# A two-block transformer kernel: projections spread evenly over the stick-breaking stream, gate rows made by transfers, and the second half's squares moved into the stream

## The chip, the cores and the metric

The kernel runs on one core of one Trainium2 chip. The metric is device time in microseconds, lower is better. TensorE (PE) multiplies, VectorE (DVE) and ScalarE (ACT) do the element-wise work, GpSimd (POOL) splits some weights, and SyncE (SP) issues most transfers.

## What is computed

Two transformer blocks are run one after the other on 1024 rows of width 1024. The first one has pooling, sliding-window attention, a feed-forward part and a gate. The second one is the one that matters here, and within it the stick-breaking attention and the mixing:

```python
def stick_breaking_attention(q, k, v):
    ...
        logits = jnp.einsum("bqhd,bkhd->bhqk", q[:, q_start:k_end],
                            k[:, :k_end]).astype(jnp.float32) * scale
        strict = (q_start + jnp.arange(SB_BLOCK))[:, None] > jnp.arange(k_end)[None, :]
        log_beta = jax.nn.log_sigmoid(logits)
        log_keep = jnp.where(strict, jax.nn.log_sigmoid(-logits), 0.0)
        log_tail = lax.cumsum(log_keep, axis=3, reverse=True) - log_keep
        weights = jnp.where(strict, jnp.exp(log_beta + log_tail), 0.0).astype(v.dtype)
        outs.append(jnp.einsum("bhqk,bkhd->bqhd", weights, v[:, :k_end]))

def hybrid_layer(x, c_act, w_ada, b_ada, w_in, rel_bias, g_a, g_b, w_out, ...):
    mod = c_act @ w_ada + b_ada
    shift_mix, scale_mix, gate_mix, shift_ffn, scale_ffn, gate_ffn = jnp.split(mod, N_MOD, axis=-1)
    h = modulate(rms_norm(x), shift_mix, scale_mix)
    proj = h @ w_in
    ...
    mixed = jnp.concatenate([rms_norm(oa) * g_a, rms_norm(ob) * g_b], axis=-1) @ w_out
    x = x + gate_mix[:, None, :] * mixed
    h = modulate(rms_norm(x), shift_ffn, scale_ffn)
    ...
    x = x + gate_ffn[:, None, :] * ((jax.nn.silu(gate) * val) @ w_down)
```

`oa` is a banded attention of 8 heads, `ob` the stick-breaking attention of 8 heads. `gate_mix` and `gate_ffn` are one number per output column, so the kernel needs them as rows that stand in all 128 partitions.

## The kernel before

Every engine has its own program, written out by hand; the order of work is the order of the code, and semaphores join the engines. A float32 product is made of three passes over operands that were split into a high and a low part (`passes`, lines 792 to 794): high by high, high by low, low by high. ScalarE or GpSimd makes the high part, VectorE subtracts to make the low part.

**The banded attention** (`outputs2`, `turn2`, `scores2`) runs 64 steps. Beside it `jobs2` computes the projections of the next pair of heads, by the table `PLAN_A`.

**The stick-breaking attention** runs NS = 96 steps, NB = 24 for each of four pairs of heads (pair 0 is steps 0 to 23, pair 3 steps 72 to 95). A step is one block of 128 queries by 128 to 512 keys for one head. In step s TensorE turns the weights of step s-2 (`turn3`, line 1355), multiplies those of step s-4 with the values (`outputs3`, lines 1371 and 1373), then does the filler work of the step, and in odd steps computes the logits of the next two (`scores3`, line 1340). ScalarE takes two sigmoids (`signs`) and copies the turned weights (`turned_hi`, wt_hi). VectorE runs a scan and a product for step s-1 (`tails`, lines 2436 and 2440) and subtracts for step s-3 (`turned_lo3`, line 2445, wt_lo). So one thing waits on another in a ring: logits, sigmoids, scan, transpose, copy, subtraction, output.

**The filler in steps 0 to 71** is the projection of the next pair (`jobs2` with `PLAN_B`): 48 products for a pair, each three matmuls over 512 columns, and two transposes (kind T) that turn the columns of V. `PLAN_B = job_plan(JOBS2, 0, 21, NB)` puts the 48 products into the first 21 of 24 steps, in the order V, Q, K, and T into steps 22 and 23. `job_hi` (ACT) and `job_lo` (DVE) copy each finished half out.

**The filler in steps 72 to 96** (`beside3`) is the first half of the mixing. In step 72 `spread_gate` multiplies `diag` (16 diagonal blocks that VectorE makes in step 71, line 2490) by ones, which leaves `gate_mix` as a row in all partitions; ScalarE copies it to `mix_gate`. In steps 73 to 76 TensorE turns eight blocks of `oa` (`turn_mixed`, line 1389), in steps 77 to 92 it multiplies (`first_half_row`, 16 pieces of 12 matmuls), and VectorE scales and adds (`first_half_sum`, lines 2478 and 2481). The mixing's weights are split by `mix_weight_hi` and `mix_weight_lo` (line 2469) in steps 70 to 73 and 93 to 96, four each, and four more blocks are turned in steps 93 to 96.

**After step 99** the second half of the mixing follows: `second_row(0)` and `(1)`, four blocks turned, a second `spread_gate` for `gate_ffn`, `second_row(2)` to `(7)`, while ScalarE squares the rows of `ob` (`ob_square`, line 1914), takes a root (line 1920) and VectorE a reciprocal (`rsq_b`). `second_sum(r)` (line 2538) needs `rsq_b` and frees the PSUM buffer that `second_row(r+2)` fills.

## Time and profile before

| what | value |
|---|---|
| median of 3 runs | 2686.29 us (2685.44 to 2689.0) |
| the profiled execution, its own time | 2674.91 us |
| its span in the trace | 2673.1 us |
| TensorE busy | 96% of the span |
| VectorE busy | 57% |
| ScalarE busy | 30% |
| granted TensorE clock, mean | 0.966 of full speed |

The profiled execution is 11.4 us (0.4%) shorter than the median of the timed runs. All times of the trace below are microseconds from the span's start. The stick-breaking stream lies between 1533 and 1874.

### The profile page before, as it was taken

The page shows a single profiled execution, that of the slowest core. Times are in us where ns is not written, and L with a number is a line of the kernel's source. Part 1 is how long each engine was busy: PE and PEld are TensorE (multiplying, and loading weights), DVE is VectorE, ACT ScalarE, POOL GpSimd, SP SyncE. Part 2 cuts the span into 40 slices and gives each one's busy share as a digit, 9 for nine tenths or more (in the row PEclk, how much of TensorE's full clock was granted, in tenths as well). Part 3 has the DMA queues.
Part 4 walks back from the last instruction along what each step waited for, and adds up shares of the span by engine and source line. Part 5 has one row for each costly group of instructions (what it writes and reads, how often), then busy time and mean ns, then how long its engine had stood idle before and what let it go on. Part 6 is the DMA issues. An engine that isn't in the chain of part 4 may idle for free.

```text
span 2673.1 us, 32589 instructions
## 1 busy us (share of the span) xinstructions
PE 2577.2 (96%) x12528; PEld 2129.4 (80%) x12528; DVE 1530.2 (57%) x2335; ACT 794.3 (30%) x1357; POOL 189.3 (7%) x94
## 2 busy tenths in 40 slices
PE   8999999999999999998999999979999999999998
PEld 6777787888888888787788878767778888888886
DVE  6658265444444437646455477778467455556566
ACT  2235041111111112535443354544542121212122
POOL 6302400000000000001222200000000000000000
PEclk9976999999999999998999999989899999999999
DMA  4401603222332234013111000021011121212111
GB/s 122 34 9 64 87 20 107 92 83 78 94 92 82 81 93 121 26 46 115 32 34 35 24 25 17 17 95 32 17 56 56 40 63 31 63 31 63 31 55 71
DMA packets 199209, 156.00 MB, mean 58 GB/s; under 512 B 54073, under 2 KB 174401, under 8 KB 199105
## 3 DMA queue, kind: packets, MB, share of 16 engines
q1 hardware_dynamic: 180976, 123.88, 16.3%
q10 hardware_dynamic: 18128, 30.71, 4.3%
q8 instruction: 67, 1.10, 0.2%
q14 instruction: 38, 0.30, 0.0%
HBM read 146.18 MB, written 11.55 MB: 59 GB/s over the span
## 4 chain that ended last, share of the span: by engine, by line
PE 88%; DVE 5%; ACT 2%; DMA 2%; issue 2%; POOL 1%; SPq 1%; ACTq 0%; DVEq 0%; PEldq 0%; POOLq 0%
PE pd L792 26%; PE pd L794 25%; PE pd L793 25%; PE pt L1293 1%; PE pd L1340 1%; PE pt L1355 1%; PE pt L1371 1%; PE pd L1262 1%; DMA raw<-in_w_out 1%; PE pt L792 1%; PE pt L1310 1%; PE pt L1373 1%; PE pt L812 1%; PE pt L794 1%; PE pt L793 1%
## 5 line engine op out<-in xcount | busy, mean ns | idle before, releaser
L792 PE MATMUL pd<-actT_hi,st_hi 128*128 128x512 f32 x1872 | 752.2, 402 | 6.0 <-DVE st_lo L2217 3.6
L794 PE MATMUL pd<-actT_hi,st_lo 128*128 128x512 f32 x1872 | 735.9, 393 | 0.0
L793 PE MATMUL pd<-actT_lo,st_hi 128*128 128x512 f32 x1872 | 735.6, 393 | 0.0
L792 PEld LDWEIGHTS pd<-actT_hi,st_hi 128*128 128x128 f32 x1872 | 356.2, 190 | 76.7 <-ACT evac L1541 3.8
L794 PEld LDWEIGHTS pd<-actT_hi,st_lo 128*128 128x128 f32 x1872 | 355.3, 190 | 76.3
L793 PEld LDWEIGHTS pd<-actT_lo,st_hi 128*128 128x128 f32 x1872 | 356.4, 190 | 67.3
L792 PE MATMUL pd<-mv_hi,hid_hi 128*128 128x512 f32 x864 | 337.1, 390 | 3.2 <-DVE acc L2530 1.5
L794 PE MATMUL pd<-mv_hi,hid_lo 128*128 128x512 f32 x864 | 336.2, 389 | 0.0
L793 PE MATMUL pd<-mv_lo,hid_hi 128*128 128x512 f32 x864 | 336.2, 389 | 0.0
L1674 ACT ACTIVATE mv_hi<-raw 128x1024 fp32r<-128x1024 f32 x54 | 55.9, 1056 | 603.2 <-PE pd L794 477.9
L1541 ACT ACTIVATE evac<-pd 128x1024 f32<-128x1024 f32 x76 | 77.9, 1024 | 452.5 <-PE pd L794 452.5
L2180 DVE TENSOR_TENSOR acc<-acc,pd 128x1024 f32<-128x1024 f32 x72 | 87.9, 1221 | 191.2 <-PE pd L794 191.1
L792 PEld LDWEIGHTS pd<-mv_hi,hid_hi 128*128 128x128 f32 x864 | 162.2, 188 | 38.7 <-DVE acc L2530 3.0
L794 PEld LDWEIGHTS pd<-mv_hi,hid_lo 128*128 128x128 f32 x864 | 162.2, 188 | 33.8
L793 PEld LDWEIGHTS pd<-mv_lo,hid_hi 128*128 128x128 f32 x864 | 162.2, 188 | 33.3
L2217 DVE TENSOR_TENSOR st_lo<-raw,st_hi 128x1024 fp32r<-128x1024 f32 (+1 forms) x83 | 103.5, 1249 | 115.9 <-ACT st_hi L1674 110.3
L731 POOL TENSOR_TENSOR st_hi<-raw,ones 128x1024 fp32r<-128x1024 f32 x27 | 66.4, 2458 | 1190.9 <-PE pd L794 1175.9
L2529 DVE TENSOR_TENSOR gated<-pd,row_b 128x1024 f32<-128x1024 f32 x48 | 58.8, 1225 | 103.7 <-PE pd L794 103.4
L2436 DVE TENSOR_TENSOR_SCAN tail<-keep,tail 128x512 f32<-128x512 f32 (+3 forms) x96 | 97.2, 1013 | 24.6 <-ACT keep L1845 24.1
L1674 ACT ACTIVATE st_hi<-raw 128x1024 fp32r<-128x1024 f32 (+1 forms) x83 | 89.0, 1075 | 52.8 <-DMA raw<-in_w_ff 19.1
L2590 DVE TENSOR_SCALAR cv<-evac,cw,cb 128x1024 f32<-128x1024 f32 x44 | 35.7, 812 | 119.0 <-ACT evac L1541 117.9
L2217 DVE TENSOR_TENSOR mv_lo<-raw,mv_hi 128x1024 fp32r<-128x1024 f32 x54 | 65.0, 1223 | 60.4 <-ACT mv_hi L1674 59.1
(343 smaller groups left out, 3792.4 us busy)
## 6 DMA issues: line engine op xcount, KB each, us to landing
raw<-in_w_ff SPq DMA_DIRECT2D x64, 512.0 KB, 3.9
ada_raw<-in_w_ada ACTq DMA_DIRECT2D x64, 384.0 KB, 3.2
raw<-in_w_up SPq DMA_DIRECT2D x44, 512.0 KB, 3.8
raw<-in_w_in SPq DMA_DIRECT2D x30, 512.0 KB, 3.7
raw<-in_w_down SPq DMA_DIRECT2D x22, 512.0 KB, 3.3
acc<-in_x SPq DMA_DIRECT2D x16, 512.0 KB, 8.8
raw<-in_w_out SPq DMA_DIRECT2D x12, 512.0 KB, 3.3
raw<-in_w_ple_gate SPq DMA_DIRECT2D x8, 512.0 KB, 3.8
```

The lines of the kernel that those rows point to most:

```text
L731: pool.tensor_tensor(hi.rearrange("p (k n) -> p k n", n=P), src.rearrange("p (k n) -> p k n", n=P), ones[:, :].unsqueeze(1).to_broadcast([ ...
L792: pe.matmul(out_ap, a_hi, b_hi, start=start, stop=False, skip_group_check=check)
L793: pe.matmul(out_ap, a_hi, b_lo, start=False, stop=False, skip_group_check=check)
L794: return pe.matmul(out_ap, a_lo, b_hi, start=False, stop=stop, skip_group_check=check)
L812: last = pe.transpose(pt[:, job % 4, r * P:(r + 1) * P], src[:, half * 4 + r, kt * P:(kt + 1) * P], ident[:, :])
L1541: act.activation(buf[:, t % 2, :], pd[:, t % 2, :], func, **kw).then_inc(t_free, 1)
L1674: act.activation(hi, src, ACT.Copy).then_inc(split_hi, 1)
L2180: return dve.tensor_tensor(acc[:, r, :], acc[:, r, :], pdr(r), ALU.add)
L2217: dve.tensor_tensor(lo, src, hi.bitcast(F32), ALU.subtract).then_inc(w_ready, 1)
L2436: link(dve.tensor_tensor_scan(tail[:, f % 2, c1 - n:c1][:, ::-1], kept, kept, tail[:, f % 2, c1:c1 + 1], ALU.mult, ALU.min))
L2529: link(dve.tensor_tensor(gt[:, :], pdr(r), row_gate[:, :], ALU.mult))
L2590: link(dve.tensor_scalar(y, u, cw[:, 2, ds(f, 1)], cb[:, ds(f, 1)], ALU.mult, ALU.add))
```

## The change

1. `jobs2(0, 5 + s // NB, PLAN_B...)` is replaced by `jobs3(s)`: two products in every one of the steps 0 to 71, in the order Q, K, V. The first T comes in step 21 of a pair, the second in step 25, which is step 1 of the next pair. `BANK3` says which half of the PSUM buffer a job uses. The order in which weight units are loaded follows.
2. `diag`, `spread_gate` and ScalarE's two copies go. VectorE signals `mod_rdy` when the modulation columns are ready; SP writes both gates' columns to DRAM (`gate_rows`) and later reads each back into all partitions (`mix_gate`, `row_b`).
3. The mixing's weights are split in steps 72 to 75 and 94 to 97, the blocks of `oa` are turned in steps 74 to 77, the 16 pieces run in steps 78 to 93, and the four blocks of `ob` are turned in steps 94 to 97.
4. The squares of rows 0 to 3 of `ob` move into ScalarE's steps 88 to 91; those of rows 4 to 7 stay behind the stream. The root and the reciprocal are replaced by VectorE's `inverse_roots` (14 small instructions), once in step 99 and once ahead of `second_sum(4)`.
5. In the banded attention's first pair, the four products of step 1 move to step 0.

```diff
+        JOBS3 = [("Q", 0), ("Q", 1), ("K", 0), ("K", 1), ("V", 0), ("T", 0), ("V", 1), ("T", 1)]
+        BANK3 = (0, 1, 0, 1, 0, 0, 1, 1)
...
+        def stick_jobs(s):
+
+            at = [(s - 25, 7), (s - 21, 5)]
+            jobs = [(5 + t // NB, e, "T", e // 7, KT - 1) for t, e in at if t % NB == 0 and 0 <= t < 3 * NB]
+            if 0 <= s < 3 * NB:
+                e, k = (0, 1, 2, 3, 4, 6)[s % NB // 4], s % 4 * 2
+                jobs += [(5 + s // NB, e) + JOBS3[e] + (k + n,) for n in range(2)]
+            return jobs
...
-        PLAN_B = job_plan(JOBS2, 0, 21, NB)
...
                     if (i, c) == (0, 3):
+                        sp.wait_ge(mod_rdy, 1)
+                        for n in range(2):
+                            sp.dma_start(bass.AP(gate_rows, n * D, [[1, P], [P, KT]]),
+                                         modT[:, 16 + 24 * n:24 + 24 * n]).then_inc(gate_out, 16)
                         sp.wait_ge(back_cp, KT)
...
             for c, (u, slot, _, _) in enumerate(SEG["out2"]["rows"]):
+                if c == 0:
+                    sp.wait_ge(gate_out, 32)
+                    sp.wait_ge(oa_sq, 8)
+                    sp.dma_start(mix_gate[:, :], bass.AP(gate_rows, 0, [[0, P], [1, D]])).then_inc(mix_gate_in, 16)
...
+            def jobs3(s):
+
+                for q, e, kind, half, k in stick_jobs(s):
+                    hi, lo, bank = 4 * NJ1 + NJ2 * q, 4 * NJ1 + NL2 * q, BANK3[e]
+                    if kind == "T":
+                        pe.wait_ge(jb_hi, hi + e)
...
+                            done = {"Q": half - 1 if q > 5 else 0, "K": 1 + half, "V": 3 + half}[kind]
+                            pe.wait_ge(jb_lo, lo + done)
+                        last = product(bank, (3 * q + "QKV".index(kind) + 1) % 2, half, k)
...
-                    jobs2(0, 1 + z // 16, PLAN_A[z % 16])
+                    jobs2(0, 1 + z // 16, PLAN_A[1] if z == 0 else [] if z == 1 else PLAN_A[z % 16])
...
-                if s == 72:
-                    pe.wait_ge(jb_lo, 4 * NJ1 + NL2 * 8)
-                    pe.wait_ge(diag_rdy, 1)
-                    spread_gate(0, pd[:, 0, :])
...
+                            pe.wait_ge(jb_lo, 4 * NJ1 + NL2 * 8)
...
-            spread_gate(8, pt[:, 0:2, :].rearrange("p a b -> p (a b)"))
...
+                if 88 <= s < 92:
+                    if s == 88:
+                        act.wait_ge(o_rows, 14)
+                    ob_square(s - 88, ob_junk[:, :])
...
+                if s == 99:
+                    dve.wait_ge(ob_sq, 4)
+                    inverse_roots(rsq_b[:, 0:4], ssq[:, 8:12], HB)
...
             for r in range(1, RT):
+                if r == 4:
+                    dve.wait_ge(ob_sq, 8)
+                    inverse_roots(rsq_b[:, 4:8], ssq[:, 12:16], HB)
                 second_sum(r)
```

**TensorE at the end of a pair.** This is TensorE's program before, in steps 71 and 72, from the outputs of step 71 on. The rows with `v_cols` are the transposes T, those with `stick` turn3, `wt_hi` and `wt_lo` outputs3, `k_hi2b` scores3.

```order
L1373 MATMUL pt<-v2a,wt_lo 128x64
L975 MATMUL pd<-ident,v_cols 128x128 x4
L1340 MATMUL pd<-k_hi2b,q_hi2b 128x128 x2
L1340 MATMUL pd<-k_lo2b,q_hi2b 128x128 x2
L1340 MATMUL pd<-k_hi2b,q_lo2b 128x128 x2
L1346 MATMUL pd<-drop_r,ident_r 128x128 x2
L1355 MATMUL pt<-ident,stick 128x128 x4
```

And this is the same place in the changed kernel.

```order
L1418 MATMUL pt<-v2a,wt_lo 128x64
L818 MATMUL pd<-actT_hi,st_hi 128x512
L819 MATMUL pd<-actT_lo,st_hi 128x512
L820 MATMUL pd<-actT_hi,st_lo 128x512
L818 MATMUL pd<-actT_hi,st_hi 128x512
L819 MATMUL pd<-actT_lo,st_hi 128x512
L820 MATMUL pd<-actT_hi,st_lo 128x512
L1385 MATMUL pd<-k_hi2b,q_hi2b 128x128 x2
L1385 MATMUL pd<-k_lo2b,q_hi2b 128x128 x2
L1385 MATMUL pd<-k_hi2b,q_lo2b 128x128 x2
L1391 MATMUL pd<-drop_r,ident_r 128x128 x2
```

Two products now stand where the last transpose T stood; the same holds for the two steps ahead of it, and T follows in step 73, behind the outputs.

**VectorE around step 72.** This is VectorE's program before, steps 71 and 72. `w_lo` is a low part of a mixing weight, `v2b` that of a T.

```order
L2436 SCALAR_TENSOR_TENSOR tail<-keep,tail 128x512
L2440 TENSOR_TENSOR stick<-stick,tail 128x512
L2445 TENSOR_TENSOR wt_lo<-pt,wt_hi 128x512
L2084 TENSOR_TENSOR v2b<-pd,v2b 128x4x128
L2490 TENSOR_SCALAR diag<-ident,modT 128x128 x16
L2469 SCALAR_TENSOR_TENSOR w_lo<-raw,gab,w_hi 128x1024
L2436 SCALAR_TENSOR_TENSOR tail<-keep,tail 128x512
L2440 TENSOR_TENSOR stick<-stick,tail 128x512
L2445 TENSOR_TENSOR wt_lo<-pt,wt_hi 128x512
L2084 TENSOR_TENSOR v2b<-pd,v2b 128x4x128
L2469 SCALAR_TENSOR_TENSOR w_lo<-raw,gab,w_hi 128x1024
```

In the changed kernel steps 72 to 74 read as follows.

```order
L2461 TENSOR_TENSOR wt_lo<-pt,wt_hi 128x512
L2485 SCALAR_TENSOR_TENSOR w_lo<-raw,gab,w_hi 128x1024
L2452 SCALAR_TENSOR_TENSOR tail<-keep,tail 128x128
L2456 TENSOR_TENSOR stick<-stick,tail 128x128
L2461 TENSOR_TENSOR wt_lo<-pt,wt_hi 128x512
L2485 SCALAR_TENSOR_TENSOR w_lo<-raw,gab,w_hi 128x1024
L2452 SCALAR_TENSOR_TENSOR tail<-keep,tail 128x128
L2456 TENSOR_TENSOR stick<-stick,tail 128x128
L2461 TENSOR_TENSOR wt_lo<-pt,wt_hi 128x512
L2100 TENSOR_TENSOR v2b<-pd,v2b 128x4x128
L2485 SCALAR_TENSOR_TENSOR w_lo<-raw,gab,w_hi 128x1024
```

The diagonal blocks are gone, and the weights and the last T stand two steps later, beside narrower scans.

**VectorE at the end of the stream.** These are the changed kernel's rows behind the last weight; before, the rows with `rsq` were one reciprocal, and it stood behind the rows of `rows_56`.

```order
L2479 TENSOR_TENSOR actT_lo<-pd,actT_hi 128x512
L2461 TENSOR_TENSOR wt_lo<-pt,wt_hi 128x512
L2479 TENSOR_TENSOR actT_lo<-pd,actT_hi 128x512
L2467 TENSOR_SCALAR rsq_v<-ssq 128x4
L2468 TENSOR_SCALAR rsq_b<-rsq_v 128x4
L2470 TENSOR_TENSOR rsq_t<-rsq_b 128x4
L2471 TENSOR_TENSOR rsq_t<-rsq_t,rsq_v 128x4
L2472 TENSOR_SCALAR rsq_t<-rsq_t 128x4
L2473 TENSOR_TENSOR rsq_b<-rsq_b,rsq_t 128x4
```

The last four of these rows come three times, and the additions to the rows of `ob`, on which `second_row(0)` waits, come only after them.

## Rows read from the trace of the kernel before

**Rows 1.** Stretches of the stream: length, PE, PEld, DVE, ACT, POOL, PEclk, DMA.

```profile
1603.00:1680.90 77.90, 76.24 (x465) 62.14 (x464) 57.48 (x87) 39.28 (x89) 0.00 (x0) 0.93 0.07 21
1680.90:1752.10 71.20, 70.94 (x457) 57.58 (x456) 54.02 (x84) 37.13 (x86) 0.00 (x0) 1.00 0.03 9
1752.10:1789.10 37.00, 23.53 (x143) 19.76 (x143) 27.80 (x56) 16.11 (x35) 0.00 (x0) 0.77 0.45 170
1789.10:1852.90 63.80, 63.80 (x369) 51.96 (x369) 53.60 (x77) 22.11 (x49) 0.00 (x0) 1.00 0.00 1
1852.90:1873.60 20.70, 15.52 (x93) 13.91 (x91) 17.98 (x23) 11.91 (x19) 0.00 (x0) 0.74 0.34 102
1873.60:1901.50 27.90, 23.43 (x104) 18.96 (x104) 9.20 (x13) 14.09 (x29) 0.00 (x0) 0.87 0.04 10
```

**Rows 2.** TensorE's timeline: start, us, instruction, [idle before <- releaser].

```profile
1275.18 0.39 PE L1262 MATMUL pd<-k_hi2a,q_hi2a 64*128 64x256 f32 x2 [2.71 <-DVE nmx L2383]
...
1602.09 0.63 PE L1355 MATMUL pt<-ident,stick 128*128 128x128 f32 x4 [1.66 <-DVE wt_lo L2445]
...
1762.55 3.78 PE L1379 MATMUL pd<-diag,ones 128*128 128x128 f32 x16 [6.51 <-DVE v2b L2084]
...
1782.73 0.77 PE L792 MATMUL pd<-w_hi,actT_hi 128*128 128x512 f32 x1 [2.46 <-DVE actT_lo L2463]
...
1789.81 0.48 PE L792 MATMUL pd<-w_hi,actT_hi 128*128 128x512 f32 x1
...
1792.65 0.49 PE L1355 MATMUL pt<-ident,stick 128*128 128x128 f32 x3
...
1890.63 1.95 PE L1379 MATMUL pt<-diag,ones 128*128 128x128 f32 x16
...
1901.51 0.79 PE L792 MATMUL pd<-w_hi,actT_hi 128*128 128x512 f32 x1 [3.44 <-DVE gated L2538]
```

**Rows 3.** VectorE's timeline in steps 71 and 72, same columns.

```profile
1754.97 3.22 DVE L2490 TENSOR_SCALAR diag<-ident,modT 128x128 f32<-128x128 f32 x16
...
1759.29 1.28 DVE L2436 TENSOR_TENSOR_SCAN tail<-keep,tail 128x512 f32<-128x512 f32 x1
1760.61 0.69 DVE L2440 TENSOR_TENSOR stick<-stick,tail 128x512 f32<-128x512 f32 x1
1761.21 0.68 DVE L2445 TENSOR_TENSOR wt_lo<-pt,wt_hi 128x512 fp32r<-128x512 f32 x1
1761.82 0.68 DVE L2084 TENSOR_TENSOR v2b<-pd,v2b 128x512 fp32r<-128x512 f32 x1
1762.41 1.28 DVE L2469 SCALAR_TENSOR_TENSOR w_lo<-raw,gab,w_hi 128x1024 fp32r<-128x1024 f32 x1
```

**Rows 4.** VectorE alone in steps 73 to 78: length, busy, PEclk, DMA.

```profile
1763.60:1784.44 20.84, 15.71 (x30) 0.83 0.45 169
```

**Rows 5.** Two stretches, columns as in rows 1, for the granted clock.

```profile
1768.00:1780.00 12.00, 9.07 (x74) 7.49 (x74) 9.96 (x19) 8.77 (x23) 0.00 (x0) 1.00 0.40 140
1780.00:1788.00 8.00, 5.54 (x18) 4.06 (x16) 4.37 (x8) 0.82 (x2) 0.00 (x0) 0.57 1.02 414
```

**Rows 6.** VectorE's timeline, first of 14 `inverse_roots` instructions, and what follows them.

```profile
1582.21 0.16 DVE L2451 TENSOR_SCALAR rsq_v<-ssq 128x8 f32<-128x8 f32 x1
...
1585.05 1.28 DVE L2436 TENSOR_TENSOR_SCAN tail<-keep,tail 128x512 f32<-128x512 f32 x1
```

**Rows 7.** ScalarE's timeline behind the stream.

```profile
1892.62 1.03 ACT L1953 ACTIVATE row_b<-pt 128x1024 f32<-128x1024 f32 x1 [1.19 <-PE pt L1379]
...
1896.75 1.99 ACT L1674 ACTIVATE st_hi<-raw 128x1024 fp32r<-128x1024 f32 x2
```

**Rows 8.** Transfers: KB each, median us from issue to landing; and SP's wait.

```profile
rows<-x_mid SPq DMA_DIRECT2D x1, 4096.0 KB, 13.0
...
b_gate<-in_b_ple_gate SPq DMA_DIRECT2D x1, 4.0 KB, 6.4
...
SPq L643 <- ACT acc L1732: 21.5, 1, 21.5
```

More of the change, by code:

```diff
@@ L383, in build @@
         m2_rms = sem("m2_rms")
-        ob_rms = sem("ob_rms")
         m2_rinv = sem("m2_rinv")
@@ L1375, in outputs3 @@
                 last.then_inc(b_pv, 1)
-            def spread_gate(n0, bank):
-                for n in range(8):
-                    last = pe.matmul(bank[:, n * P:(n + 1) * P], ones[:, :], diag[:, n0 + n, :], start=True, stop=True)
-                last.then_inc(bc_mm, 1)
             def turn_mixed(b, bank):
@@ L2071, in job_lo @@
                     dve.wait_ge(jb_hi, i * (2 * NJ2) + (n + e + 1))
-                    bank = 0 if one else half
+                    bank = 0 if one else BANK3[e] if q is not None and q != "alone" and q >= 5 else half
                     src = pd[:, q_slot if kind == "Q" else 0, bank * HB:(bank + 1) * HB]
```

189 lines of the change are left out of this document (88 added, 101 removed).

## The prediction

> **What bounds the kernel now.** I read the stretches of the stream first. In pair 2 TensorE is busy for 70.94 of 71.20 us at full clock, and in steps 78 to 92 for 63.80 of 63.80 us, while VectorE has 54.02 and 53.60 us of work there [rows 1]. So TensorE sets the time in the middle of a pair, and spreading or removing VectorE's work there brings nothing. The reader is to look at the four rows where this fails: pair 1 (clock 0.93), steps 72 to 77 (TensorE busy 23.53 of 37.00 us, clock 0.77), steps 93 to 99 (15.52 of 20.70) and the first second rows (23.43 of 27.90). Second I read TensorE's timeline for what ended each gap [rows 2]: VectorE each time, its wt_lo at a pair's end, v2b (the last T) in step 72, actT_lo ahead of the first piece of the mixing, gated in the second rows, nmx at the start of the banded attention. Third, VectorE's own rows around step 72 [rows 3, 4].
>
> **The sum, part by part.**
>
> *a. The first pair of the banded attention.* TensorE stood 2.71 us for VectorE's nmx [rows 2]. Four products now lie in that gap; a product is three matmuls, and 12 matmuls took 1792.65 - 1789.81 = 2.84 us [rows 2], so 0.71 us each and 2.8 us for four. The gap is filled, but the four no longer cover the first transposed block on its way through ScalarE and VectorE; the nearest row for such a subtraction is 0.68 us, for 512 columns [rows 3], and I allow 0.8 us for the narrow copy and subtraction together. Net 2.0 us; the clock may stay up as well, so I take 2.4. Bounds: 0.3 (the products start late, behind the last T) and 3.3.
>
> *b. The ends of pairs 0 and 1.* A 512-wide step costs VectorE 1.32 + 0.60 + 0.61 = 2.53 us from start to start (scan, product, wt_lo) [rows 3]. TensorE's own part without filler is below that: pair 2 is 71.2 / 24 = 3.0 us a step, 1.4 of it products, which leaves 1.6 in the mean and, as an estimate, 1.8 in a wide step. So in the last three steps of a pair, which held no product, TensorE ran into wt_lo. There are two such waits of this size, 1.66 us each, at the ends of pairs 0 and 1 [rows 2]. With two products in every step, TensorE's wide step is 3.2 us, over VectorE's 2.5. In steps 20 to 24 VectorE also has a T (0.6) and, last, a weight (1.2): five times 2.53 and 1.8 is 14.5 us against 16. I count 3.3 us gained. The 48 products and six transposes are the same in number and cost nothing new.
>
> *c. The clock behind the first of these waits.* Pair 1's busy time is 76.24 us against pair 2's 70.94 [rows 1], the same instructions at a granted clock of 0.93: 5.3 us, which is a stretch at 1.2 GHz that came after the 1.66 us gap at 1602 [rows 2]. The like gap at the end of pair 1 had no such stretch behind it: pair 2 ran at 1.00. Without the gap I take 5.1 us back; lower bound 0, since one of two gaps did it and a run without it gains nothing.
>
> *d. Steps 72 to 78.* Before, 37.00 us from the logits of step 72 to step 78 [rows 1]: the 6.51 us wait for v2b, which came late because VectorE first made diag (3.22 us) and split weights, then the `diag` matmuls (3.78 us, at half clock), then waits for actT_lo, the last 2.46 us [rows 2, 3]. Now VectorE alone sets this stretch. Its program of steps 73 to 78 before took 15.71 us of work [rows 4]; the changed one adds two weights and the last T: 15.71 + 2 x 1.19 + 0.60 = 18.7 us, starts from rows 3. By my estimate VectorE begins it 1.5 us after the logits of step 72 are begun (logits, then the first sigmoid), and waits 0.9 us for T in step 74: ScalarE's `signs(74)` stands ahead of T's copy and needs the logits that TensorE issues behind T. So the eighth block is ready after 21.1 us, the first piece of 12 matmuls ends at 21.1 + 2.84 = 23.9, and step 78's attention is then done too, which before ends only at 1789.81, 0.7 us later [rows 2]. Gain 37.7 - 23.9 = 13.8. By the same count TensorE has some 6 us of gaps in there, in four waits; that the clock then falls over the first piece, as it did before in [rows 5], costs up to 2.8. I take 11; bounds 8 and 14.
>
> *e. The gate rows by transfer.* The columns are ready long before SP needs them, and SP issues the two writes where it stood 21.5 us for ScalarE's acc [rows 8]. Each has 1024 elements of four bytes; the read of the same shape landed after 6.4 us [rows 8]. Behind them on SP wait the eight writes of x_mid and the next weights. Cost nothing, covered by the 21.5 us; without that cover it would be some 6 to 13 us. The reads back are issued when VectorE's weight splits of step 49 let SP go on, over 20 steps ahead of their use, and row_b is used only in the feed-forward part. The 4096 KB read of x_mid lands after 13.0 us [rows 8]; it is issued at the outputs of step 75, about 8 us into (d), and needed at 23.9, so 3 us of cover are left.
>
> A rule speaks against this: each element goes out alone. The Trainium skill, "DMA: Bandwidth & Descriptors" (the list of numbers at its head and its table of patterns), says that a strided last dimension becomes one descriptor for each element and that under 512 bytes the engine reads, modifies and writes. No row here shows such a write to DRAM; the sum goes by the 6.4 us row and its cover.
>
> *f. The end of the stream.* From the end of the last piece VectorE has, by the changed order and the starts of [rows 3], four weights 4.8, two wide scans and products 3.8, four wt_lo 2.4 and four actT_lo 2.4 (as v2b), then the 14 instructions of `inverse_roots`, 1585.05 - 1582.21 = 2.84 [rows 6]; `first_half_sum` and the two additions I put at 2.3, as four instructions of 0.6. That is 18.5 us, and one step's attention (1.8 us) now lies ahead of the last piece. Before it was 20.70 us [rows 1]. 18.5 + 1.8 = 20.3: I take 0.2 gained, bounds -2 and 2.
>
> *g. The second rows.* Before, `second_row(3)` began at 1901.51, behind 3.44 us of waiting for gated [rows 2]. The second `diag` matmuls (1.95 us) go, so `second_row(2)` starts 2 us earlier; but gated comes from ScalarE's chain: row_b's copy begins at 1892.62 after waiting 1.19, and the squares and the root end at 1896.75 [rows 7], where the weights begin. The wait and the copy (1.19 + 0.92) and the small root (0.2) fall out, so all behind moves up 2.3 us. The wait of TensorE stays, 3.1 us. The second `inverse_roots` (2.84) stands between `second_sum(3)` and `(4)`, where a row of TensorE is eight products, 5.7 us, and VectorE's two 1024-wide instructions (2.4, as w_lo) and the roots make 5.4: nothing. Gain 2.3; bounds 0 and 5.
>
> Sum: 2.4 + 3.3 + 5.1 + 11 + 0 + 0.2 + 2.3 = 24.3 us. The profiled execution would be 2674.9 - 24.3 = 2650.6. It lies 11.4 us under the median of the timed runs, whose gap no row explains; I let the gain stand on the median: 2686.3 - 24.3 = 2662.0.
>
> **The rivals.**
>
> 1. *The clock takes part of it back.* TensorE still has gaps in steps 74 to 77 and 94 to 99, and short ones may appear elsewhere. For it: every stretch at 1.2 GHz followed a gap [rows 1, 2]. Against it: from 1768 to 1780, with gaps and many transposes, the clock was 1.00 [rows 5]. If (c) is lost to another stretch and (d) gives 8: 24.3 - 5.1 - 3 = 16 us, 2670. Chance 0.27. The Trainium skill, "TensorE: Matmul & The Clock Gate" (Part 4: PE-mode transpose), says that transposes do not count as activity for the gate; the eight turned blocks of steps 74 to 77 would then be at half clock whatever the gaps. The row of 1768 to 1780 speaks against it, as that stretch held the same turned blocks.
>
> 2. *The clock stays up everywhere.* The stretches at half clock behind the gaps at 1782, 1873 and 1901 go too: 2.8 for the piece, 0.13 of 27.90 us [rows 1] = 3.6 for the second rows, and as much as 2 behind 1901: 8.4 on top, 32.7 us, 2654. Chance 0.12.
>
> 3. *VectorE becomes the bound* in the last steps of a pair, because T, the weight and wide scans now meet there: (b) and (c) come back as new waits, and (d) starts late by about 2 us. 24.3 - 8.4 - 2 = 14 us, 2672. The margin worked out in (b) is 1.5 us in five steps, and VectorE's program is about 76% full in pair 2 [rows 1]. Chance 0.10.
>
> 4. *Slower: the gate columns' write.* If the writes hold up SP's queue, x_mid lands late, ScalarE waits for it before the first projection, and TensorE behind it. The cover is 21.5 us [rows 8]; each us beyond is lost. It outweighs the 24.3 from a landing after 46 us, seven times the 6.4 of the row; at 57 us the kernel takes 2686.3 + 11 = 2697. Chance 0.02.
>
> That the change brings only what lies in (a), (e) and (g), under 6 us, because TensorE's work were the bound in steps 72 to 78 as well, is excluded by the 13.5 us in which it stood there [rows 1]; for other small results I leave 0.04.
>
> **The numbers.** My forecast (24.3 us, give or take 4) has 0.45. The range for eight in ten runs from rival 2, 2653, to just beyond rival 3, 2674. A measurement of this kernel can tell about 0.2%, 5.4 us. Faster by more than that: 0.45 + 0.27 + 0.12 + 0.10, less a little for noise, 0.93; same 0.04; slower 0.03.
>
> **What would show it.** (b): no gap at 1.66 us in TensorE's timeline at the pairs' ends, and three pairs of some 71 us each. (c): clock 1.00 over pairs 0 to 2. (d): steps 72 to 78 in about 24 us, with VectorE busy nearly all the time, and waits for actT_lo of about 2 us. (e): mix_gate and row_b wait for nobody, x_mid lands in time. (f): the last additions behind `inverse_roots`, TensorE waiting about 1 us for them. (g): a gap of about 3 us for gated. Wrong I would be if VectorE showed gaps of its own in (d), that is if the ring through ScalarE or the transfers of weights and not its work set the pace, or if the half-clock stretches moved to dense products.

## The result and the profile after

The changed kernel took 2667.57 us (median of 6 runs, 2653.37 to 2676.73), the kernel before, beside it, 2685.86 (2677.46 to 2689.0). The ratio is 0.9933, interval 0.9906 to 0.996: 18 us less, between 11 and 25. The forecast was 2662.0 in a range of 2653 to 2674. These are six runs each. Measured again (first experiment), the changed kernel took 12 us less by the ratio, and the kernel before took 2672.23, 2673.76 and 2670.62 us beside the later versions, 12 to 15 us less than here; so 18 may be too much. Two of all runs took far longer, one of version `both` 3628.22 us, at a granted clock of 0.646, and one of the kernel before beside it 6433.47 us; the ratios leave them out.

The profiled execution took 2653.37 us, with a span of 2651.6 and a mean granted clock of 0.973; before it was 2674.91, 2673.1 and 0.966. The spans differ by 21.5 us, and the table splits that at marks that both traces have. The marks: A0, the first logits of the banded attention; S0, S24, S48 and S72, the logits of that step of the stream; R0, the first matmul of the mixing's first half; R15, the end of its 16th piece; SR0 and SR3, the start of `second_row(0)` and `(3)`; M2, the first matmul behind the mixing. In brackets stands the time at a granted clock of 1.2 GHz.

| stretch | before | after |
|---|---|---|
| span's start to A0 | 1271.9 (112.6) | 1259.9 (81.9) |
| A0 to S0 | 261.5 (5.2) | 259.0 (0) |
| S0 to S24 | 70.6 (5.8) | 73.2 (6.8) |
| S24 to S48 | 76.8 (9.5) | 72.9 (0) |
| S48 to S72 | 71.3 (0) | 72.5 (0) |
| S72 to R0 | 30.6 (12.2) | 29.3 (21.8) |
| R0 to R15 | 70.1 (4.9) | 69.5 (5.5) |
| R15 to SR0 | 20.8 (10.9) | 19.6 (12.0) |
| SR0 to SR3 | 27.9 (7.4) | 24.8 (5.1) |
| SR3 to M2 | 33.7 (5.6) | 32.7 (3.4) |
| M2 to the end | 737.9 (8.3) | 738.1 (8.8) |

So 12.0 of the 21.5 us lie ahead of A0, where the change has nothing but two writes on SP's queue; 30.7 us less at 1.2 GHz are enough for them: the 12 matmuls of the mixing's first piece took 5.25 us at that level (changed kernel, 1766.86 to 1772.11) and 2.84 at full clock [rows 2], so 30.7 us at half clock can cost 14 us. In what was changed, A0 to M2, 9.7 us were gained (663.3 to 653.6), where the forecast had 24.3: 2.5 between A0 and S0, nothing in the three pairs, 7.1 between S72 and M2. The three pairs of the stream, at which a third of the forecast was aimed, take 218.7 and 218.6 us.

The stretches of the changed kernel, columns as in [rows 1]:

```profile
1518.90:1592.10 73.20, 69.38 (x413) 54.98 (x412) 54.33 (x97) 40.51 (x97) 0.00 (x0) 0.95 0.05 15
1592.00:1665.00 73.00, 71.36 (x457) 57.25 (x456) 56.33 (x86) 38.31 (x87) 0.00 (x0) 1.00 0.10 30
1665.00:1737.50 72.50, 71.21 (x457) 57.30 (x456) 55.05 (x85) 37.29 (x86) 0.00 (x0) 1.00 0.05 16
1737.50:1766.90 29.40, 22.72 (x127) 19.64 (x126) 22.49 (x37) 17.83 (x39) 0.00 (x0) 0.63 0.58 215
1774.00:1836.00 62.00, 62.00 (x358) 50.48 (x357) 52.27 (x75) 21.75 (x52) 0.00 (x0) 1.00 0.00 1
1836.00:1856.00 20.00, 14.37 (x84) 12.92 (x82) 17.78 (x34) 11.41 (x18) 0.00 (x0) 0.70 0.39 121
1856.00:1880.80 24.80, 21.15 (x88) 16.84 (x88) 9.16 (x12) 9.57 (x18) 0.00 (x0) 0.90 0.06 20
```

Rows two and three are pairs 1 and 2. Both run at full clock, yet TensorE is busy 71.3 of 72.8 us where pair 2 before had 70.94 of 71.20: each pair now has 1.3 to 1.6 us of waits inside. The fourth row is the stretch on which term (d) rests: no engine is full there, VectorE has 22.49 us of work in 29.40, and the clock is 0.63. (Before, the mixing's first piece lay in step 77, now it lies in step 78, so S72 to R0 and S72 to R15 hold one step's attention more than before and R15 to SR0 one less; only S72 to SR0 compares like with like, 121.5 before and 118.5 now.) TensorE's timeline at the waits:

```profile
1261.48 0.47 PE L818 MATMUL pd<-actT_hi,st_hi 128*128 128x512 f32 x1 [1.03 <-DVE v2a L2100]
1266.44 0.30 PE L1338 MATMUL pt<-ident,prob 128*128 128x128 f32 x1 [1.14 <-DVE pT_lo L2405]
...
1546.21 0.63 PE L1400 MATMUL pt<-ident,stick 128*128 128x128 f32 x4 [0.87 <-DVE wt_lo L2461]
...
1572.89 0.63 PE L1400 MATMUL pt<-ident,stick 128*128 128x128 f32 x4 [2.85 <-DVE wt_lo L2461]
...
1746.17 1.97 PE L1429 MATMUL pd<-ident,rows 128*128 128x128 f32 x8 [1.91 <-DVE v2b L2100]
...
1753.80 0.69 PE L1391 MATMUL pd<-drop_r,ident_r 128*128 128x128 f32 x2
...
1756.45 1.97 PE L1429 MATMUL pd<-ident,rows 128*128 128x128 f32 x8 [1.25 <-DVE actT_lo L2479]
...
1763.30 0.69 PE L1391 MATMUL pd<-drop_r,ident_r 128*128 128x128 f32 x2
...
1766.86 0.77 PE L818 MATMUL pd<-w_hi,actT_hi 128*128 128x512 f32 x1 [1.51 <-DVE actT_lo L2479]
...
1772.11 0.61 PE L1400 MATMUL pt<-ident,stick 128*128 128x128 f32 x3
...
1880.80 0.50 PE L818 MATMUL pd<-w_hi,actT_hi 128*128 128x512 f32 x1 [2.64 <-DVE gated L2555]
```

The 1.66 us waits at the ends of pairs 0 and 1 [rows 2] are gone, and so is the 6.51 us wait for v2b. In their place stand a wait of 0.87 us in every pair (pair 0's at 1546.21) and one of 2.85 us at 1572.89, in step 18, in the middle of pair 0. In the three pairs TensorE stood 3.5 us before and 6.7 us now, summed over the gaps of its timeline. What VectorE did ahead of the 2.85 us wait:

```profile
1565.83 0.69 DVE L2097 TENSOR_TENSOR k_lo2b<-pd,k_hi2b 128x512 fp32r<-128x512 f32 x1 [2.48 <-ACT k_hi2b L1609]
1566.44 0.16 DVE L2467 TENSOR_SCALAR rsq_v<-ssq 128x8 f32<-128x8 f32 x1
...
1569.26 1.22 DVE L2080 TENSOR_TENSOR st_lo<-raw,st_hi 128x1024 fp32r<-128x1024 f32 x1
1570.41 1.28 DVE L2452 TENSOR_TENSOR_SCAN tail<-keep,tail 128x512 f32<-128x512 f32 x1
```

VectorE stands 2.48 us for ScalarE's high part of K, because the second half of K now ends in step 15; then come the 14 instructions of `inverse_roots` for the first squares (2.82 us, in step 16, where the code had them before too), then a weight (1.22); only then the scan that TensorE needs. Before, the roots stood between plain steps, with no wait and no weight beside them (a scan at 1580.49 ahead, one at 1585.05 behind); now they follow the end of a job. The 0.87 us waits have the same form with Q's end and a weight, without the roots.

Of the transfers, the queue's view (columns as in [rows 8]):

```profile
rows<-x_mid SPq DMA_DIRECT2D x1, 4096.0 KB, 14.0
...
mix_gate<-gate_rows SPq DMA_DIRECT2D x1, 512.0 KB, 4.6
row_b<-gate_rows SPq DMA_DIRECT2D x1, 512.0 KB, 5.9
...
gate_rows<-modT SPq DMA_DIRECT2D x2, 4.0 KB, 11.5
...
SPq L662 <- ACT acc L1762: 20.2, 1, 20.2
```

### The profile page after: what moved, and what is told of

It reads as the page before. It is cut to its first block, busy times and chain, and to the rows that moved or that the text cites. A ratio compares the mean times of both kernels' runs of the same rounds, so it can differ in the third digit from the quotient of the medians.

```text
span 2651.6 us, 32495 instructions
## 1 busy us (share of the span) xinstructions
PE 2557.0 (96%) x12496; PEld 2112.1 (80%) x12496; DVE 1529.8 (58%) x2345; ACT 789.4 (30%) x1353; POOL 188.4 (7%) x94
## 4 chain that ended last, share of the span: by engine, by line
PE 87%; DVE 6%; ACT 2%; issue 2%; DMA 2%; SPq 1%; POOL 1%; ACTq 0%; DVEq 0%; PEldq 0%; POOLq 0%
PE pd L818 25%; PE pd L820 25%; PE pd L819 25%; PE pt L1338 1%; PE pd L1385 1%; DMA raw<-in_w_out 1%; PE pd L1307 1%; PE pt L1400 1%; PE pt L818 1%; PE pt L1416 1%; PE pt L1355 1%; PE pt L838 1%; PE pt L1418 1%; PE pt L820 1%; PE pt L819 1%
## 5 line engine op out<-in xcount | busy, mean ns | idle before, releaser
L1573 ACT ACTIVATE evac<-pd 128x1024 f32<-128x1024 f32 x76 | 77.9, 1024 | 451.9 <-PE pd L820 451.9
L1704 ACT ACTIVATE st_hi<-raw 128x1024 fp32r<-128x1024 f32 (+1 forms) x83 | 89.0, 1075 | 51.3 <-DMA raw<-in_w_ff 19.6
```

The lines of the kernel that those rows point to most:

```text
L1573: act.activation(buf[:, t % 2, :], pd[:, t % 2, :], func, **kw).then_inc(t_free, 1)
L1704: act.activation(hi, src, ACT.Copy).then_inc(split_hi, 1)
```

## The experiments

The stages below are those of the table above, read from the profiled execution of each kernel. They repeat within 0.2 us between kernels that share a stage and its clock; the timed ratios have intervals that are 0.3 to 0.7% wide (9 to 18 us), so the stages tell the parts apart, not the medians.

**The changed kernel again, and its parts alone.** One comparison of the same kernel, then three with a part undone or alone.

> The changed kernel once more. Its first profile was 21.5 us shorter than the one before, but 12 us of that lay ahead of 1214 us, in work that both kernels share, where 24 us fewer ran at 1.2 GHz. Theory A (the change is worth what lies in its own stretches, some 9 to 13 us, and the rest was the clock's luck in shared work): ratio 0.995 to 0.9965, and in a new profile the stretch from the logits of step 0 to those of step 72 is again 218 to 220 us, as before. Theory B (the change is worth the 18 us of the medians): ratio 0.9925 to 0.994, and the stretch of the three pairs is 212 to 215 us in a profile without bad luck.

2661.84 us against 2672.23, ratio 0.9955 (0.9937 to 0.9973), that is 12 us less; by this, and by the three pairs at 218.7 us, it is theory A. From S0 on each stage is the same as in the first trace within 0.2 us, the 2.85 us wait too. But A0 to S0 took 265.9 us, with 17.1 us at 1.2 GHz. The two traces in the same stretch, behind the same wait of 1.04 us for pT_lo at its start (first row the changed kernel's first trace, second row this one):

```profile
1321.00:1339.00 18.00, 17.36 (x112) 14.88 (x111) 10.24 (x41) 6.84 (x20) 0.00 (x0) 1.00 0.16 46
```

```profile
1321.00:1339.00 18.00, 17.76 (x78) 16.36 (x79) 7.86 (x27) 6.19 (x16) 0.17 (x1) 0.53 0.23 67
```

The same program behind the same wait once kept 2.4 GHz and once fell for 17 us, which cost 6.9 us. Of the 11 traces with this order of the first pair (two of the changed kernel, one of each of nine versions), two fell there and nine did not.

**Only the spread undone:** the changed kernel with the 48 products in the first 21 steps of each pair, and T in steps 19 and 22.

```diff
-                e, k = (0, 1, 2, 3, 4, 6)[s % NB // 4], s % 4 * 2
-                jobs += [(5 + s // NB, e) + JOBS3[e] + (k + n,) for n in range(2)]
+                jobs = [(q, e, "T", e // 7, KT - 1) for at, e in ((19, 5), (22, 7)) if u == at]
+                for g in range(48):
+                    if g * 21 // 48 == u:
+                        e = (0, 1, 2, 3, 4, 6)[g // 8]
+                        jobs.append((q, e) + JOBS3[e] + (g % 8,))
```

> The changed kernel with its 48 products of a pair packed into 21 of 24 steps again, same order Q, K, V, T in steps 19 and 22. Theory A (the even spread moves TensorE's waits from the pair's end to its steps 8 and 18 and gains nothing): three pairs in 217 to 220 us, waits of 1.7 us return at the ends of pairs, those of 0.87 us near step 9 go, ratio within 0.001 of the changed kernel. Theory B (the even spread is worth the 3.3 us of the old waits and the clock behind them): 3 to 8 us slower than the changed kernel, ratio to the kernel before 0.996 to 0.998.

2666.13 us, ratio 0.9967 (0.9947 to 0.9986), which the timing alone can't tell from the changed kernel's. The three pairs, S0 to S72:

```profile
1524.40:1747.35 222.95, 217.76 (x1329) 176.48 (x1329) 165.11 (x264) 117.39 (x271) 0.00 (x0) 0.95 0.07 20
```

They take 223.0 us, 4.3 more than with the even spread, although TensorE stands only 5.2 us in them rather than 6.7: the clock is at 1.2 GHz for 20.5 us and not for 6.8. The waits moved as theory A said (1.8 us at the ends of pairs 0 and 1, none of 0.87), the price is theory B's. So in these traces what the even spread brings comes through the clock, and it is paid for with waits. The trace before was a lucky one for this comparison: the next two kernels below keep its uneven spread, and their pairs took 220.5 and 221.4 us, with 19.6 and 21.4 us at 1.2 GHz, since in them a stretch of 6 to 7 us at that level followed the second 1.66 us wait too. Against the mean of the three, 220.2, the even spread gains 1.5 us and not nothing. Single traces do not fix it closer: one with the even spread, `after_fill` below, took 221.1.

**Only the gate rows by transfers,** put into the kernel before (its stream, its order of squares and roots).

```diff
-        diag = place("diag", [P, 16, P], F32, R_S + 4 * KB)
...
+        gate_rows = nc.dram_tensor("gate_rows", [2, D], F32)
...
+                        sp.wait_ge(mod_rdy, 1)
+                        for n in range(2):
+                            sp.dma_start(bass.AP(gate_rows, n * D, [[1, P], [P, KT]]),
+                                         modT[:, 16 + 24 * n:24 + 24 * n]).then_inc(gate_out, 16)
```

> The kernel before with the gate rows made by transfers and nothing else. Theory A (diag and its matmuls are the largest part of the gain): the stretch from the logits of step 72 to step 78 falls from 37.0 to 28 to 30 us, the second rows lose 2 us, together 8 to 11 us, ratio 0.996 to 0.997. Theory B (the moved steps carry the gain; without them the wait for the last T stays): under 5 us, ratio 0.998 to 1.0.

2666.59 us, ratio 0.9976 (0.9954 to 0.9998). Its S72 to R0:

```profile
1749.90:1777.50 27.60, 19.80 (x106) 17.79 (x106) 22.34 (x37) 15.47 (x34) 0.00 (x0) 0.63 0.40 149
```

S72 to SR0 falls from 121.5 to 117.9 us (118.5 as changed), SR0 to SR3 from 27.9 to 25.3, SR3 to M2 from 33.7 to 32.7. S72 to M2 is 7.2 us less together, between the two theories, and as much as the whole change brings there (7.1). So behind S72 the transfers are the gain; moving the weights and turned blocks one step on, beside the last T, brought nothing.

**Only the squares in the stream and VectorE's roots,** put into the kernel before.

```diff
+                if 88 <= s < 92:
+                    if s == 88:
+                        act.wait_ge(o_rows, 14)
+                    ob_square(s - 88, ob_junk[:, :])
...
-                act.activation(rms[:, c], ssq[:, c], ACT.Sqrt, bias=eps[:, 1:2], scale=1.0 / HB).then_inc(ob_rms, 1)
...
+                if s == 99:
+                    dve.wait_ge(ob_sq, 4)
+                    inverse_roots(rsq_b[:, 0:4], ssq[:, 8:12], HB)
```

> The kernel before with only the squares of rows 0 to 3 in the stream and VectorE's inverse roots for both halves. Theory A (ScalarE's root cost 0.2 us, and VectorE's 14 instructions delay the last additions by about 1.3): within 2 us of the kernel before, ratio 0.9993 to 1.0007. Theory B (the squares held up the second rows): 3 us faster, ratio 0.9988, with the wait for gated under 1 us.

2678.33 us, ratio 1.0015 (0.9998 to 1.0032): SR0 to SR3 0.6 us less, R15 to SR0 0.2 more, and nothing else that the change touches (the third pair took 3.0 us more with 6.8 us at 1.2 GHz). It is theory A. The squares cost nothing where they were: before, ScalarE made those of rows 0 to 3 from 1873.8 to 1876.8 us and stood 9.74 us for the next turned block soon after.

**The roots in step 26.**

```diff
-                if s == 16:
+                if s == 26:
                     dve.wait_ge(oa_sq, 8)
```

> The changed kernel with the inverse roots of the first squares made in step 26 instead of step 16; nothing else differs. Theory A (the roots, 2.82 us of VectorE's time between 1566.44 and 1569.26, make wt_lo late at the end of pair 0, and the half-clock stretch of 6.8 us follows that 2.85 us wait): the steps 0 to 24 fall from 73.2 us to 69.5 to 70.7, with no low clock in them, and the kernel is some 3 us faster than the changed one, unless the roots then open a like gap in step 26. Theory B (VectorE is late there anyway, because T, a weight and wide steps meet at the end of a pair): the waits of about 0.9 us stay and the steps 0 to 24 stay above 72 us.

2657.11 us against 2673.76, ratio 0.9939 (0.9917 to 0.9962). S0 to S24:

```profile
1530.40:1599.50 69.10, 67.79 (x414) 53.51 (x413) 52.08 (x81) 40.53 (x97) 0.00 (x0) 0.98 0.06 16
```

69.1 rather than 73.2 us, the 2.85 us wait now 0.36, and the stretch of 3.4 us at 1.2 GHz behind it gone; in steps 24 to 48 the roots cost 0.3 us. The cause is theory A's, and the gain a little more than its 69.5 to 70.7. The expectation had put both stretches at 1.2 GHz, 6.8 us, down to that wait; the other 3.4 us stand at the first us of the stream and stayed. The 0.87 us waits stayed, as theory B said of them: they are Q's end and a weight ahead of a scan, and the roots have no part in them.

**The logits of steps 74, 76 and 78 first,** ahead of the turned blocks and products of the step before them in the code.

```diff
+                early = s in (73, 75, 77)
+                if early:
+                    scores3(s + 1)
                 jobs3(s)
                 beside3(s)
-                if s % 2 and s + 1 < NS:
+                if s % 2 and s + 1 < NS and not early:
                     scores3(s + 1)
```

> The changed kernel with the logits of steps 74, 76 and 78 issued ahead of the turned blocks and products of steps 73, 75 and 77 instead of behind them. Theory A (the ring turned blocks, logits behind them, ScalarE's signs, actT_hi, actT_lo sets the pace of steps 73 to 78): from the logits of step 72 to the first piece of the mixing 29.4 us fall to 25 to 27, and VectorE's idle spells of 2.87 and 3.20 us in there shrink under 1 us each. Theory B (VectorE's own work sets the stretch, as predicted): under 1 us of change. Theory C (TensorE's own work at 1.2 GHz sets it): under 1.5 us of change, and TensorE's waits of 1.91, 1.25 and 1.51 us move to other instructions with the same sum.

2652.08 us, ratio 0.9934 (0.9913 to 0.9956). S72 to R0, and TensorE's last wait in it:

```profile
1741.20:1765.10 23.90, 19.37 (x126) 17.20 (x126) 22.45 (x37) 18.36 (x39) 0.00 (x0) 0.79 0.57 210
```

```profile
1765.10 0.47 PE L818 MATMUL pd<-w_hi,actT_hi 128*128 128x512 f32 x1 [1.79 <-DVE actT_lo L2482]
```

VectorE's work is the same (22.45 us, 22.49 as changed), and the stretch is 5.4 us shorter, more than the 2.4 to 4.4 that theory A expected; VectorE is now 94% busy in it, and its waits of 2.87 and 3.20 us are 0.54 at most. Theory A. (The clock was also higher, 0.79 and not 0.63; what that is worth is measured below.) The ring that this opened can be read in the changed kernel on two engines. ScalarE first, then VectorE:

```profile
1754.31 0.49 ACT L1874 ACTIVATE keep<-pd 128x384 f32<-128x384 f32 x1 [3.82 <-PE pd L1391]
...
1763.81 0.60 ACT L1874 ACTIVATE keep<-pd 128x512 f32<-128x512 f32 x1 [4.22 <-PE pd L1391]
```

```profile
1755.70 1.29 DVE L2479 TENSOR_TENSOR actT_lo<-pd,actT_hi 128x512 fp32r<-128x512 f32 x2 [2.87 <-ACT actT_hi L1894]
...
1765.42 1.29 DVE L2479 TENSOR_TENSOR actT_lo<-pd,actT_hi 128x512 fp32r<-128x512 f32 x2 [3.20 <-ACT actT_hi L1894]
```

ScalarE's `signs(76)` (keep, 1754.31) stands 3.82 us for the logits whose last matmul is the `drop_r` row at 1753.80; those logits are issued behind the turned blocks at 1750.64; behind `signs` on ScalarE stands actT_hi of blocks that were turned already; VectorE stands 2.87 us for that (1755.70), and TensorE 1.25 us for VectorE (1756.45). Every two steps it goes round again.

**Both edits.**

> Both of these edits together: the inverse roots in step 26, and the logits of steps 74, 76 and 78 issued first. If the two causes are separate, the gains add: 2.5 to 3.5 us in the steps 0 to 24 and 2.5 to 4 us from the logits of step 72 to the first piece, so 5 to 7.5 us under the changed kernel in the part behind the start of the banded attention. If one clock history carries both (a stretch at 1.2 GHz saved at one place comes at another), the sum is under 4 us.

2656.44 us, ratio 0.9929 (0.9902 to 0.9956). S0 to S72 214.9 (218.6 as changed) and S72 to R15 92.5 (98.9): the gains add, 10.2 us together, above the expected 5 to 7.5: the order had given 5.4 us to R0 already, and the pieces behind R0 got 0.9 us from the clock too. The median does not show it (2654.98 without the run of 3628.22), and is no lower than that of the order alone; the profiled execution had the 17.1 us at 1.2 GHz between A0 and S0, as in the trace above.

**More work on VectorE:** an addition of 1024 columns in steps 76 and 78, in two kernels.

```diff
+                    if s in (76, 78):
+                        dve.wait_ge(mix_gate_in, 16)
+                        gate = mix_gate.rearrange("p (h c) -> p h c", c=HB)
+                        link(dve.tensor_tensor(half_gated[:, :, :], gate, gate, ALU.add))
```

> The changed kernel with one 1024-wide addition more on VectorE, whose result nothing uses, in each of the steps 76 and 78, ahead of the subtractions for the turned blocks (2 x 1.2 us by the 1024-wide rows of w_lo). It tests the step of the prediction that VectorE's work alone sets the stretch from step 72 to the first piece. Prediction's view: the 29.4 us from the logits of step 72 to the first piece grow by 2.4 us. Ring view (turned blocks, logits behind them, ScalarE): both additions fall into idle spells of VectorE (2.87 and 3.20 us) and the stretch grows by under 0.4 us.

> The same two additions on VectorE in the kernel that issues the logits of steps 74, 76 and 78 first. There VectorE has no idle spell over 0.4 us between the second and the last turned block, so if it is the bound once the ring is opened, the 23.9 us from the logits of step 72 to the first piece grow by 1.8 to 2.4 us; if TensorE or ScalarE still sets the pace, by under 1 us.

S72 to R0 in the changed kernel with the load, in the changed kernel with the logits first and the load:

```profile
1738.00:1767.50 29.50, 22.63 (x127) 19.60 (x126) 24.74 (x39) 17.90 (x39) 0.00 (x0) 0.63 0.58 214
```

```profile
1735.60:1761.30 25.70, 17.39 (x127) 15.28 (x126) 24.67 (x39) 18.15 (x39) 0.00 (x0) 0.87 0.65 245
```

In the changed kernel 2.3 us more of VectorE's work cost nothing: 29.5 us, which another trace of the same kernel without load also had. With the logits first they cost 1.8 us (23.9 to 25.7), although the clock happened to be higher. VectorE's waits of 2.87 and 3.20 us fell to 1.81 and 2.14, so the additions went into them. So VectorE's work did not set this stretch in the changed kernel, and does once the ring is open. Single runs took 2653.73 and 2644.81 us.

**Extra products in a gap.** Three products (nine matmuls) in step 74, ahead of the wait for v2b; the turned block overwrites their result.

```diff
+                        if b == 0:
+                            for k in range(3):
+                                passes(pd[:, 0, 0:HB], st_hi[:, 0, k, :], st_lo[:, 0, k, :], actT_hi[:, k, 0:HB],
+                                       actT_lo[:, k, 0:HB], True, True)
```

> The changed kernel with only the three extra products of step 74 (nine matmuls in the gap before the turned blocks, result overwritten), the logits of steps 74, 76 and 78 where the change has them. With the three kernels measured it makes a table of order and clock: from the logits of step 72 to the end of the 16th piece 98.9 us as changed, 92.4 with the order alone, 91.0 with both. If the order alone matters: 98 to 100.5 us, with a clock of 1.2 GHz for 20 us or more. If the clock alone explains what the order won (a short gap less keeps it up): under 94 us with under 12 us of low clock.

S72 to R0:

```profile
1752.10:1781.10 29.00, 22.46 (x135) 18.82 (x135) 22.45 (x37) 17.64 (x39) 0.00 (x0) 0.74 0.58 218
```

It took 29.0 us with 15.0 at 1.2 GHz (29.3 and 21.8 without), and 98.5 to R15; the single run took 2667.63 us. 6.8 us less at half clock were worth 0.3 us: TensorE's speed was not what set the stretch, its order was, as the first of the two expectations had it. In this trace the 2.85 us wait in step 18 was followed by 6.8 us at 1.2 GHz and not 3.4.

> Both edits, and in step 74, ahead of the wait for v2b, three products more (nine matmuls, 2.1 us at full clock) whose result is overwritten, so that TensorE has no long gap in front of the turned blocks. Theory A (the gap of 1.9 us behind the logits of step 72 is what brings the clock to 1.2 GHz for 27.3 us): the clock stays at 2.4 GHz at least to the second block, and the stretch from the logits of step 72 to the first piece is 2 us or more shorter than with both edits alone, although it holds more work. Theory B (the turned blocks themselves, or all the short gaps of steps 74 to 77, bring the clock down): the clock falls within 5 us of the same place, and the stretch is 0 to 2 us longer than with both edits alone.

2653.08 us, ratio 0.9919 (0.9888 to 0.995). S72 to R0 24.0 us with 6.8 at 1.2 GHz, as against 23.9 and 10.2 with both edits alone, though it holds nine matmuls more; R0 to R15 67.0 rather than 68.6, since nothing there fell to half clock. To R15 1.5 us are won (91.0 against 92.5). This is neither theory's full case: the clock still fell, later and for less.

**Extra products at three gaps:** both edits, the fill in step 74, three products ahead of the turned weights of step 94, and three ahead of `second_row(3)`.

```diff
+                if s == NS:
+                    pe.wait_ge(b_stick, NS)
+                    (q_hi, q_lo), (k_hi, k_lo) = att2[1]["q"], att2[1]["k"]
+                    for k in range(3):
+                        passes(pd[:, 1, 0:HB], q_hi[:, 0:P], q_lo[:, 0:P], k_hi[:, 0:HB], k_lo[:, 0:HB], True, True)
...
             second_row(2)
+            for j in range(3):
+                passes(pt[:, 0, :], actT_hi[:, 4 + j, 0:P], actT_lo[:, 4 + j, 0:P], w1_hi[:, j, 0:HB],
+                       w1_lo[:, j, 0:HB], True, True)
             second_row(3)
```

> The best kernel so far (roots in step 26, logits of 74, 76 and 78 first, three extra products in step 74) with three extra products each at two more places where TensorE waits over 2.5 us: ahead of the turned weights of step 94 (3.02 us, of which the products are to fill 2.1) and ahead of the fourth second row (2.64 us); their results are overwritten. If the gap before brings the clock down at each place: 0 to 3 us of low clock from the 16th piece to the first second row instead of 13, worth 1 to 3 us, and from the first to the fourth second row and behind it 1 to 2.5 us less. If VectorE sets these stretches whatever the clock: the low clock goes but the stretches keep 19.6 and 24.1 us. If something else brings the clock down: no change in either. Of the whole kernel I expect 0.9925 to 0.9895 of the time before.

2644.57 us against 2670.62, ratio 0.9899 (0.9865 to 0.9933), the fastest version and, by its stages too, better than both kernels (A0 to M2 638.7 us; 653.6 as changed, 663.3 before). S72 to R0, the stretch around step 94, and behind `second_row(3)`:

```profile
1734.20:1757.30 23.10, 17.64 (x135) 14.80 (x134) 22.28 (x37) 18.30 (x39) 0.00 (x0) 1.00 0.63 233
...
1824.00:1844.00 20.00, 14.92 (x94) 12.63 (x92) 17.78 (x34) 11.19 (x18) 0.00 (x0) 0.84 0.40 121
...
1868.00:1900.00 32.00, 31.80 (x156) 26.61 (x157) 21.34 (x40) 18.96 (x31) 0.00 (x0) 1.00 0.08 27
```

The first row is the whole of S72 to R0 at full clock, with all eight turned blocks: 23.1 us, 0.8 less than at a clock of 0.79, and VectorE busy 22.28 of them. Around step 94 the clock rose (0.70 to 0.84, 6.5 us at half clock rather than 12) and R15 to SR0 stayed 19.6 us to the tenth: there VectorE sets the time, 17.78 us of work in both. At `second_row(3)` the wait fell from 2.64 to 0.59 us, its place taken by the extra products; `second_row(3)` began no earlier for it (SR0 to SR3 24.1 us, as in the version before this one), and behind it no clock was lost: 31.1 us to M2 rather than 32.7.

## Why the forecast was right in the whole and wrong in parts

The range held the time, and the sum of 24.3 us came within 7 of what the medians show. The parts did not: A0 to M2 gave 9.7 us, and 12.0 came ahead of it. That the time lay in the range is in large part luck: measured again, the change brought 12 us, half of the sum, and of the three terms that made 19.4 of the 24.3 us, (b), (c) and (d), the traces show some 3 between them.

**Ahead of A0.** The step "I let the gain stand on the median" took no account of how much the shared work differs between executions. Its time at 1.2 GHz ahead of A0 ranges from 81.9 to 122.9 us over the profiled kernels, its length from 1257.9 to 1273.7. Three traces with the old first pair took 1271.0 us in the mean, eleven with the changed one 1264.7. Whether the changed kernels are faster there by anything but luck stays open; single traces of three do not tell it, and no mechanism was found.

**(a) first banded pair, forecast 2.4, trace 2.5.** The 2.71 us wait [rows 2] went; two waits of 1.03 and 1.14 us came, one for v2a ahead of the moved products and one for the first pT_lo (0.8 was allowed for the latter). So 0.5 us came from waits and the rest from the clock (5.2 us at 1.2 GHz to none). With the two traces that fell behind A0 counted in, eleven traces have 260.4 us in the mean, three of the old order 261.7: 1.3 us. This edit was not run alone.

**(b) pair ends, forecast 3.3 won, 3.2 lost.** The step that failed is the count over "five times 2.53 and 1.8 against 16". It counted VectorE's work in the last five steps of a pair. The two waits at the ends did go. But each end of a job puts onto VectorE, ahead of the scan, a wait for ScalarE's high part (1.6 to 2.8 us) and, at every second one, a weight. Such waits stood there before too (1.66 us for Q, 2.72 for K) and cost TensorE nothing. That with two products in each step no step is left in which TensorE does more than its share and covers them fits the experiment that undid the spread, where the 0.87 us waits were gone; it is not shown further. And the roots of step 16, which I had only used for a duration [rows 6], were not looked for in the new order: they now stand behind K's end. Rival 3 had the mechanism (VectorE late in the pairs), with T as its cause and the pairs' ends as its place, and both were wrong.

**(c) the clock behind the first wait, forecast 5.1, trace 3.3.** The three pairs' busy time fell from 215.1 to 211.9 us for the same instructions, with 6.8 rather than 15.3 us at half clock; 3.4 us of what is left follow the 2.85 us wait. The remark that the like gap at the end of pair 1 had no such stretch behind it held for that one trace; in two others of the same order it had (6.1 and 6.8 us). So (b) and (c) together are nil between these two traces (1.5 us against the mean of three) where 8.4 us were forecast, and moving the roots by ten steps gives 3.7 of them (214.9 us).

**(d) steps 72 to 78, forecast 11 (bounds 8 and 14), trace 3.1** (from S72 to the start of step 79 34.6 us, 37.7 before). Failed: "VectorE alone sets this stretch". Its work was sized well: for steps 73 to 78 18.7 us were forecast, and 18.8 were measured. The start was not:

```profile
1740.39 1.28 DVE L2485 SCALAR_TENSOR_TENSOR w_lo<-raw,gab,w_hi 128x1024 fp32r<-128x1024 f32 x1 [0.53 <-ACT w_hi L1901]
1741.59 0.48 DVE L2452 TENSOR_TENSOR_SCAN tail<-keep,tail 128x128 f32<-128x128 f32 x1
```

VectorE began step 73 at 1741.59, 4.05 us after S72 and not 1.5, because the scan, the product, wt_lo and the weight of step 72 stand ahead. Then it stood idle for 6.35 us where 0.9 were allowed, and the first piece took 5.25 us at half clock and not 2.84. With 0.15 from its last row to R0 that makes the 34.6 us: 4.05 + 18.8 + 6.35 + 0.15 + 5.25. What I left out is that a turned block, the logits behind it, ScalarE's `signs` and actT_hi make a ring. I had seen one turn of it (0.9 us at T in step 74) and did not go round again. The load of 2.3 us that cost nothing shows it, and the edit of the order shows its price: 5.4 us to R0 and 6.4 to R15. The transfers of weights, the other suspect of the prediction's last sentence, made ScalarE wait 1.06 and 0.38 us (w_hi at 1745.00 and 1747.52), and no wait of VectorE follows them. With the order changed and the three fills, S72 to SR0 is 109.7 us, 11.8 less than before, about what (d) and (f) had together.

The clock, rival 1's subject, was at 0.51 over the blocks and the first piece:

```profile
1744.50:1772.00 27.50, 21.61 (x84) 18.12 (x85) 18.25 (x31) 12.71 (x27) 0.00 (x0) 0.51 0.56 211
```

It fell inside the gap of 1.91 us ahead of the first turned block, at 1745.1, before any block was turned. By the rule of the Trainium skill ("TensorE: Matmul & The Clock Gate", Part 4: PE-mode transpose), that transposes do not count as activity for the gate, the turned blocks would keep it down. The trace after agrees with the rule; the one with three fills does not bear it out as the only cause: there all eight blocks ran at 1.00, in 23.1 us. In the version with the logits first the clock came back at 1759.1, ahead of the last two blocks. And what a higher clock gave was small: 0.3 us for 6.8 us less at 1.2 GHz with the ring, 0.8 us for 10.2 us less with the ring open.

**(e) the gate rows, forecast 0, right.** The two writes landed after 11.5 us and not after the 6.4 of the read of the same shape [rows 8]; the 20.2 us for which SP then stands for acc cover them. mix_gate and row_b waited for nobody, x_mid was delayed by nothing. x_mid landed at 1763.9, ahead of its first use at 1772.4. The Trainium skill ("DMA: Bandwidth & Descriptors", the list of numbers at its head) says that under 512 bytes the engine reads, modifies and writes. That the write of single elements took nearly twice the read of the same shape fits it; no run shows that this is the cause. And the removal of diag and its matmuls, which I had priced inside (d) and (g), was the best part of the change: 3.6 us from S72 to SR0 and 3.6 from there to M2, with the transfers alone.

**(f) end of the stream, forecast 0.2, trace 1.1** from R15 to SR0, one step's attention more lying ahead of it; VectorE sets it, as said: its work is 17.78 us at either clock, and the stretch 19.6 us at 0.70 and at 0.84.

**(g) the second rows, forecast 2.3, trace 3.1 and 1.0 behind it.** TensorE's wait for gated is 2.64 us, 3.1 were forecast. But (g) is the gate row's copy: the transfers alone gave 2.6, the squares and roots alone 0.6.

Of the rivals none is the case. The first gives 16 us by the loss of (c) and 3 us of (d); the medians show 18, but (c) was not lost to the clock, and (d) not to it either.

## What to carry to other kernels

Before saying that one engine sets a stretch, follow its waits round: who made the input, what is issued ahead of that, and whether you meet the first engine again. If extra work on the engine costs nothing, the engine was not the bound. Here it was a ring, and the order on the engine ahead of it in the ring was what to change.

When work is spread evenly, look for the one-off instructions (here 14 small ones) that lay under a loose part. They keep their step and can lose their cover. And compare stages, not medians, where the shared work varies by more than the change brings.
